# Row stages of a two-block transformer kernel: the first 128 tokens handled apart from the others

## The reference

```python
x = x + rmsnorm(mixed @ w_out[l], attn_post_norm[l])     # first row stage
h = rmsnorm(x, ffn_pre_norm[l])                          # goes into w_up
...
y = (gelu(gate) * up) @ w_down[l]
x = x + rmsnorm(y, ffn_post_norm[l])                     # second row stage
h = modulate(rms_norm(x, norm_gains[0, 0]), ...)         # goes into w_qkv of the second block
```

## Time and profile before

| | before |
|---|---|
| median of 3 runs | 1040.23 us (1039.89 to 1041.08) |
| the profiled execution | 1041.97 us |
| its span, first to last instruction | 1040.2 us |
| PE busy | 1023.5 us (98%) |
| DVE busy | 813.5 us (78%) |
| ACT busy | 592.8 us (57%) |
| POOL busy | 165.7 us (16%) |
| mean granted TensorE clock | 0.997 |

### The profile page before, as it was taken

How to read it: one execution, slowest core, us unless ns; L and a number is a source line. 1 busy time by engine, 2 the same in 40 slices (tenths; PEclk the granted TensorE clock), 3 DMA queues, 4 the chain that set the end, 5 groups by cost and what they waited for, 6 DMA issues and landing times.

```text
span 1040.2 us, 18418 instructions
## 1 busy us (share of the span) xinstructions
PE 1023.5 (98%) x7440; PEld 955.2 (92%) x7440; DVE 813.5 (78%) x1399; ACT 592.8 (57%) x1027; POOL 165.7 (16%) x172
## 2 busy tenths in 40 slices
PE   8999999999999999999999999999999999999997
PEld 7988898999889997999999889988999899999987
DVE  5878799999997987588999798885668676674553
ACT  5688676665446666565444455544465566544443
POOL 1000134333101200032122011201100123111010
PEclk8999999999999999999999999999999999999999
DMA  9733356776894433457997887554434536774441
GB/s 363 263 121 123 122 195 243 271 290 249 324 390 176 163 123 122 159 190 279 373 381 299 318 312 281 203 174 150 158 127 165 200 128 235 282 268 152 168 167 41
DMA packets 34129, 227.44 MB, mean 219 GB/s; under 512 B 3795, under 2 KB 4092, under 8 KB 10492
## 3 DMA queue, kind: packets, MB, share of 16 engines
q1 hardware_dynamic: 33596, 223.63, 57.5%
q0 software_dynamic: 448, 2.63, 0.6%
HBM read 225.19 MB, written 2.63 MB: 219 GB/s over the span
## 4 chain that ended last, share of the span: by engine, by line
PE 86%; DVE 9%; ACT 2%; issue 1%; DMA 0%; POOL 0%; POOLq 0%; SPq 0%; ACTq 0%; DVEq 0%
PE psum L1513 16%; PE psum L1514 16%; PE psum L1515 16%; PE psum L1557 9%; PE psum L1558 5%; DVE w_lo L2269 3%; PE psum L1582 2%; PE psum L1585 2%; PE psum L1584 2%; PE psum L1933 2%; PE psum L1935 2%; PE psum L1934 2%; ACT w_hi L827 1%; PE psum L1724 1%; DVE arena L2593 1%; PE psum L1616 1%
## 5 line engine op out<-in xcount | busy, mean ns | idle before, releaser
L2269 DVE TENSOR_TENSOR w_lo<-raw,w_hi 128x1024 fp32r<-128x1024 f32 (+2 forms) x340 | 387.1, 1160 | 134.3 <-ACT w_hi L827 129.2
L827 ACT ACTIVATE w_hi<-raw 128x1024 fp32r<-128x1024 f32 (+2 forms) x340 | 333.4, 996 | 210.0 <-PE psum L1515 82.6
L1513 PE MATMUL psum<-h_hi,w_hi 128*128 128x256 f32 (+1 forms) x1144 | 324.5, 284 | 5.6 <-DVE w_lo L2269 2.7
L1514 PE MATMUL psum<-h_hi,w_lo 128*128 128x256 f32 (+1 forms) x1144 | 321.0, 281 | 0.0
L1515 PE MATMUL psum<-h_lo,w_hi 128*128 128x256 f32 (+1 forms) x1144 | 320.6, 280 | 0.0
L1513 PEld LDWEIGHTS psum<-h_hi,w_hi 128*128 128x128 f32 x1144 | 215.4, 188 | 9.4 <-DVE w_lo L2269 5.6
L1515 PEld LDWEIGHTS psum<-h_lo,w_hi 128*128 128x128 f32 x1144 | 215.4, 188 | 0.0
L1514 PEld LDWEIGHTS psum<-h_hi,w_lo 128*128 128x128 f32 x1144 | 214.7, 188 | 0.7 <-issue 0.7
L1513 PE MATMUL psum<-hid,w_hi 128*128 128x256 f32 (+1 forms) x532 | 152.6, 287 | 0.5 <-DVE w_lo L2269 0.2
L1514 PE MATMUL psum<-hid,w_lo 128*128 128x256 f32 (+1 forms) x532 | 149.9, 282 | 0.0
L1515 PE MATMUL psum<-hid,w_hi 128*128 128x256 f32 (+1 forms) x532 | 149.9, 282 | 0.0
(11 more groups left out here) (302 smaller groups left out, 1371.3 us busy)
## 6 DMA issues: line engine op xcount, KB each, us to landing
arena<-in_ada SPq DMA_DIRECT2D x48, 1024.0 KB, 6.1
raw<-in_gu SPq DMA_DIRECT2D x44, 1024.0 KB, 6.9
raw<-in_ret_in SPq DMA_DIRECT2D x24, 1024.0 KB, 4.8
raw<-in_up SPq DMA_DIRECT2D x22, 1024.0 KB, 4.8
raw<-in_dn SPq DMA_DIRECT2D x32, 704.0 KB, 4.1
raw<-in_qkv SPq DMA_DIRECT2D x12, 1024.0 KB, 5.0
raw<-in_down SPq DMA_DIRECT2D x11, 1024.0 KB, 7.5
raw<-in_ret_o SPq DMA_DIRECT2D x8, 1024.0 KB, 4.8
```

The source lines that it names most:

```text
L827: nc.scalar.activation(w_hi[chunk % SPLIT_SLOTS][:, a:b], raw[chunk % RAW_SLOTS][:, a:b], ACT.Copy)\
L1513: nc.tensor.matmul(out, w[0], hc, start=start, stop=False, skip_group_check=True)
L1514: nc.tensor.matmul(out, w[1], hc, start=False, stop=False, skip_group_check=True)
L2269: tt(w_lo[s][:, a:b], raw[chunk % RAW_SLOTS][:, a:b], w_hi[s][:, a:b].bitcast(F32), ALU.subtract)\
```

## The change

The factor of the first 128 tokens is made as soon as their two pieces are squared: `row_mean`, `row_roots` and `row_rstd` are each called once for r = 0 and once for r = 1, on one column instead of two. The refinement has the factor 1.5 and -0.5 folded in, still four small steps. The diagonal of r = 0 moves from DVE to ACT (`first_diag`), that of r = 1 stays on DVE. PE turns all eight blocks of r = 0 first and then all of r = 1; 14 filler matmuls stand ahead in stage 0, and none ahead and 4 between the two turns in stage 1, instead of 18 ahead. The PSUM places of the turned tiles are dealt out anew, tile 7 shares a bank with tile 0 and waits for its reading, and DVE is told after tiles 0, 2, 4, 6 and 7. In `rows_by_gains` ACT squares tile 0 after rounding tile 1, tile 1 after 2, tile 2 after 4, tile 3 after 5, and tiles 4 to 7 after 7, instead of each right behind its own.

```diff
 def turned_rows(k):
-    return (tra + att)[k // 2][:, k % 2 * S:k % 2 * S + S]
+    bank, at = ((tra[0], 0), (tra[1], 0), (tra[1], S), (att[0], 0), (att[0], S), (att[1], 0), (att[1], S), (tra[0], S))[k]
+    return bank[:, at:at + S]
+TURN_ENDS = (0, 2, 4, 6, 7)
...
+def row_roots(stage, r):
+    act.wait_ge(row_ms, 2 * stage + r + 1)
+    nc.scalar.activation(row_stat[:, 6 + r:7 + r], row_stat[:, r:r + 1], ACT.Sqrt).then_inc(row_root, 1)
+def first_diag(stage):
+    act.wait_ge(row_factor, stage + 1)
+    nc.scalar.activation(row_diag_of(0), ident[:, :], ACT.Identity, scale=row_stat[:, 24:25]).then_inc(row_diag, 1)
 def mix_squares(ph):
     for r in range(2):
+        if r:
+            row_roots(0, 0)
         for n in range(2):
...
-    act.wait_ge(row_ms, 1)
-    nc.scalar.activation(row_stat[:, 6:8], row_stat[:, 0:2], ACT.Sqrt).then_inc(row_root, 1)
+    first_diag(0)
+    row_roots(0, 1)
 def row_squares(ph, i):
     for r in range(2):
+        if r:
+            row_roots(stage, 0)
         for n in range(2):
             if r == 1 and n == 1:
+                first_diag(stage)
                 act.wait_ge(half_done, 2 * (ph.chunk0 + ph.n))
...
+    row_roots(stage, 1)
 def rows_by_gains(i):
+    squares = {1: (0,), 2: (1,), 4: (2,), 5: (3,), 7: (4, 5, 6, 7)}
     for k in range(DT):
...
-        square(i, k)
+        for n in squares.get(k, ()):
+            square(i, n)
 def turn_rows(ph, i):
-    keep_busy(18, att[1])
+    if stage == 0:
+        keep_busy(14, att[1])
+    else:
+        pe.wait_ge(row_copied, 2)
+    pe.wait_ge(row_diag, 2 * stage + 1)
+    for k in range(DT):
+        turn(k, 0)
+    if stage:
+        keep_busy(4, sco[0])
     units_done(pe, ph.unit0 + ph.units)
...
+    pe.wait_ge(row_diag, 2 * stage + 2)
     for k in range(DT):
+        if k == DT - 1:
+            pe.wait_ge(row_x, DT * stage + 1)
+        ins = turn(k, 1)
+        if k in TURN_ENDS:
             ins.then_inc(row_turned, 1)
 def row_copies(ph, i):
     for r, n in ((0, 0), (0, 1), (1, 0)):
+        if r:
+            row_mean(ROW_STAGE[i], 0)
+            row_rstd(ROW_STAGE[i], 0)
 def row_residual(ph, i, gain_):
-    stt(row_stat[:, 0:2], row_stat[:, 28:30], EPS, row_stat[:, 30:32], ALU.add, ALU.add).then_inc(row_ms, 1)
-    refine(row_root, stage + 1, row_stat, 2)
-    for r in range(2):
-        ts(row_diag_of(r), ident[:, :], row_stat[:, 24 + r:25 + r], -0.5, ALU.mult, ALU.mult).then_inc(row_diag, 1)
+    if stage == 0:
+        row_rstd(0, 0)
+    row_mean(stage, 1)
+    row_rstd(stage, 1)
+    ts(row_diag_of(1), ident[:, :], row_stat[:, 25:26], 1.0, ALU.mult, ALU.mult).then_inc(row_diag, 1)
...
 def add_rows(c, first, r, g):
     for n in range(2):
+        if (c, r, n) == (3, 1, 1):
+            row_mean(0, 0)
```

More of the change, by code:

```diff
@@ L361, in build @@
             "rows_done", "row_sq", "row_copied", "row_ms", "row_root", "row_diag", "row_turned", "row_x"))
+        row_factor = sem("row_factor")
         settled_conv, settled_qk = sem("settled_conv"), sem("settled_qk")
@@ L1073, in row_squares @@
                                              scale=D ** -0.5, accum_out=row_stat[:, at:at + 1]).then_inc(row_sq, 1)
-                act.wait_ge(row_ms, stage + 1)
-                nc.scalar.activation(row_stat[:, 6:8], row_stat[:, 0:2], ACT.Sqrt).then_inc(row_root, 1)
+                row_roots(stage, 1)
                 leave(nc.scalar.activation(row_of(1, 1), row_bank(ph, 1, 1)[:, :], ACT.Copy), ph.unit0 + 1)
             def rows_by_gains(i):
+                squares = {1: (0,), 2: (1,), 4: (2,), 5: (3,), 7: (4, 5, 6, 7)}
                 for k in range(DT):
@@ L1943, in turn_rows, with turn @@
                 stage = ROW_STAGE[i]
-                keep_busy(18, att[1])
+                rows = mix_rows if stage == 0 else e0["y"]
+                def turn(k, r):
+                    return nc.tensor.matmul(turned_rows(k)[:, r * P:(r + 1) * P], rows[:, r * D + k * P:r * D + (k + 1) * P],
+                                            row_diag_of(r), start=True, stop=True)
+                if stage == 0:
[7 more added lines that the diff above has]
+                    keep_busy(4, sco[0])
                 units_done(pe, ph.unit0 + ph.units)
@@ L1947, in turn_rows @@
                     pe.wait_ge(row_y, 2)
-                else:
-                    pe.wait_ge(row_copied, 2)
-                rows = mix_rows if stage == 0 else e0["y"]
+                pe.wait_ge(row_diag, 2 * stage + 2)
                 for k in range(DT):
-                    for r in range(2):
[L1953 to L1957, removed]
+                    if k == DT - 1:
+                        pe.wait_ge(row_x, DT * stage + 1)
+                    ins = turn(k, 1)
+                    if k in TURN_ENDS:
                         ins.then_inc(row_turned, 1)
@@ L2339, in norm_h, with row_mean, row_rstd @@
                 tiles_of(i)
+            def row_mean(stage, r):
+                dve.wait_ge(row_sq, 4 * stage + 2 * (r + 1))
+                stt(row_stat[:, r:r + 1], row_stat[:, 28 + r:29 + r], EPS, row_stat[:, 30 + r:31 + r], ALU.add, ALU.add).then_inc(row_ms, 1)
+            def row_rstd(stage, r):
+                m, s, a, f = (row_stat[:, at + r:at + r + 1] for at in (0, 12, 18, 24))
+                dve.wait_ge(row_root, 2 * stage + r + 1)
+                link(nc.vector.reciprocal(s, row_stat[:, 6 + r:7 + r]))
+                link(stt(a, s, -0.5, m, ALU.mult, ALU.mult))
+                link(tt(a, a, s, ALU.mult))
+                ins = stt(f, a, 1.5, s, ALU.add, ALU.mult)
+                if r == 0:
+                    ins.then_inc(row_factor, 1)
+                else:
+                    link(ins)
             def row_copies(ph, i):
                 for r, n in ((0, 0), (0, 1), (1, 0)):
+                    if r:
+                        row_mean(ROW_STAGE[i], 0)
+                        row_rstd(ROW_STAGE[i], 0)
                     dve.wait_ge(row_sq, 4 * ROW_STAGE[i] + 2 * r + n + 1)
@@ L2353, in row_residual @@
                 stage = ROW_STAGE[i]
-                dve.wait_ge(row_sq, 4 * (stage + 1))
-                stt(row_stat[:, 0:2], row_stat[:, 28:30], EPS, row_stat[:, 30:32], ALU.add, ALU.add).then_inc(row_ms, 1)
-                refine(row_root, stage + 1, row_stat, 2)
-                for r in range(2):
-                    ts(row_diag_of(r), ident[:, :], row_stat[:, 24 + r:25 + r], -0.5, ALU.mult, ALU.mult).then_inc(row_diag, 1)
+                if stage == 0:
[3 more added lines that the diff above has]
+                ts(row_diag_of(1), ident[:, :], row_stat[:, 25:26], 1.0, ALU.mult, ALU.mult).then_inc(row_diag, 1)
                 def rest_of(k):
@@ L2365, in row_residual @@
                 for k in range(DT):
-                    if k % 2 == 0:
-                        dve.wait_ge(row_turned, DT // 2 * stage + k // 2 + 1)
+                    if k == 0 or k - 1 in TURN_ENDS:
+                        dve.wait_ge(row_turned, len(TURN_ENDS) * stage + (k + 3) // 2)
                     cut = slice(k * S, (k + 1) * S)
```

## The result

The changed kernel took 1048.53 us (median of 6 runs, 1046.95 to 1049.64), the kernel before 1040.65 us in the same rounds (6 runs, 1039.89 to 1043.87): ratio 1.0068, 95% interval 1.0057 to 1.0080, so 7.1 us slower by the ratio. Forecast was 1043.6 us with a range up to 1046.5. The sign and the first mechanism, sums that wait for POOL, came out as forecast. The clock, which the forecast expected to be kept, fell as well, and the time lies outside the range.

The account below looks back on a forecast made before the run. PE bounds most of the kernel, but DVE sets the pace from 321 to 347 us. Late sums in stage 0 (+1.7 to +2.2) and stage 1 (+1.2 to +1.75), taken as +3.4 on 1040.23, gave 1043.6 us, range 1041.3 to 1046.5.

Parts of the forecast that it names:

- the first mechanism: Both row stages: PE's sums of squares wait for POOL's additions, +1.7 to +2.2 us in stage 0, +1.2 to +1.75 in stage 1.
- Part 1: Stage 1, early factor of r = 0: factor at about 320.2, ACT's diagonal 0.4 us, diagonal of r = 1 about 322.45.
- Part 2: PE's split turn: first residual 0.5 us earlier in stage 1 (bounds 0.3 to 0.65), 0.1 in stage 0 (0 to 0.2).
- Part 3: Moved squares: last rest some 0.5 us sooner, but POOL's late additions meet DVE's splits; sums late, +3.4 us over both stages.
- the first of the two orders: POOL's fourth addition ahead of DVE's first split: split runs 7.53 to 8.67 from the first residual; stage 1 sums at 334.5.
- clock kept: The forecast's own case: both stages late by the sums, no clock fall, 1042.2 to 1044.6 us; chance 0.50.
- (b): PE stands still around the sums and the clock falls: +1.2 to +2.9 us per stage hit, 1044.8 to 1049; chance 0.17.
- (a): Sums not late, POOL slipping between DVE's work or PE's head start covering it: about 1040.2, at best 1038.6; chance 0.20.
- its weaker form: POOL's additions undisturbed by the splits, ending at 332.97 in stage 1 and 133.9 in stage 0: about 1040.2, no change.
- (c): Second addition comes ahead of the fifth rest, last rounding 0.8 us later in that stage: 1044.4 to 1045.2; chance 0.10.
- (d): Early turn brings nothing because ACT's diagonal holds the fourth square: +0.5 us, inside the forecast's range, no chance of its own.
- Slack at chunk 3: Sign: PE's 0.49 us wait for DVE at chunk 3 should stay; if gone, DVE had room and the forecast is wrong.

Follow-up runs that it names:

- e1: Changed kernel with each square again right behind its own rounding (early factor and split turn stay): 1040.54 us, ratio 0.9990 to the kernel before.
- e6: Changed kernel with DVE's split of chunk 1 in both row stages reading one operand from PSUM (that part's product wrong): 1043.35 us, ratio 1.0019.
- e2: Kernel before with only the new places of the squares: 1047.79 us, ratio 1.0072.
- e10: The changed kernel itself, unedited, run again beside e11: 1048.48 us, ratio 1.0064 to the kernel before.
- e3b: Changed kernel with 4 filler matmuls ahead of chunk 1 and 14 ahead of the sums in both row stages: ratio 1.0043 to the kernel before.
- e11: Same kernel as e3b (fillers while PE waits), timed again beside the changed kernel: 1044.36 us, ratio 1.0023 to the kernel before.
- e5: Changed kernel with squares trailing their rounding by one tile only (tiles 6 and 7 behind 7): 1043.25 us, ratio 1.0009.
- e7: e1 with 2 fillers instead of 4 between the two turns of stage 1: ratio 0.9994 to the kernel before.
- e9: Same version as e7 (e1 with 2 fillers in stage 1), timed again in more rounds: ratio 0.9997 to the kernel before.
- e4: Changed kernel with three POOL additions in the row stages, PE summing tiles 4 to 7 itself (20 one-column passes instead of 8): 1045.14 us, ratio 1.0029.
- e8: e4 with 6 fillers of 256 columns ahead of the one-column passes in each row stage: 1043.79 us, ratio 1.0037.

## Why the prediction was right on the late sums and wrong on the clock

**Part 1, the early factor: right to 0.1 us.** Forecast in before's time: factor at 320.2, first turn 320.73, second diagonal 322.45, second turn 323.0, first residual 323.46. Measured, less the 2.31 us by which the trace of after stands later: 320.16, 320.71, 322.38, 323.05, 323.47. ACT's new diagonal took 0.40 us, as taken between its two neighbours. This timeline row of ACT is the term that the earlier trace rows could only bound:

```profile
322.47 0.40 ACT L1057 ACTIVATE diag<-ident,row_stat 128x128 f32<-128x128 f32 x1 [0.24 <-DVE row_stat L2379]
```

**Part 2, the turn: right.** The residual is 0.50 earlier in stage 1 (forecast 0.5) and 0.16 in stage 0 (forecast 0.1, bound 0.2).

**Part 3, the squares: right.** The split of chunk 1 starts at 332.83, in before's time 330.52 (forecast 330.5); of this, 0.49 us is due to the squares in each stage (after against e1; forecast 0.5). POOL was first by 0.06 us, as in the first of the two orders. The forecast had the split wait its turn; in fact it starts and is stretched, 1.76 us for 1.22, and the fifth addition ends 0.60 us behind the split's end (335.19 against 334.59), just the distance of the earlier trace rows. The same again for the second split and the sixth addition (336.86 against 336.27). Sums in before's time: 334.68 in stage 1 (forecast 334.5 or 335.0) and 135.55 in stage 0 (forecast 135.4 or 135.95). Together +3.24 against +3.4.

The trace agrees with the Trainium skill (SBUF — State Buffer, "Who interferes with whom") on the kind of conflict, and e6 shows that it goes away with a PSUM operand. The forecast set DVE's loss of 0.49 us against the 0.74 of a whole addition and made a difference of it, but a loser can only be held for what is left of the other's operation when it starts. Read so, both engines pay alike in this trace: the first split starts with 0.68 us of the addition left and loses 0.54 (1.76 instead of 1.22), the fifth addition starts with 0.94 us of the split left and loses 0.79 (1.53 instead of 0.74). The row that seems to break the order, POOL's at 462.92 ahead of two splits, starts inside a DVE operation with two SBUF operands (L2601, 462.76 to 463.23), and so second.

**The step that failed: "clock kept" as the likeliest case, and (b) at 0.17.** The forecast itself laid out PE's work around the sums: 0.8 us of waiting, 0.46 of work, another 1.8 to 2.3 of waiting (in the trace of after 0.57 and 0.55 of waiting, then 1.73 in both stages). It also had the earlier trace rows, in which PE was busy for 2.58 of 3.45 us and half clock followed. The layout leaves PE far less busy than the row in which the clock had fallen, so by the rows at hand (b) deserved far more than 0.17, and nothing was put forward against it. It happened in both stages of the trace of after, in both of e2 and in both of e10, in each case behind a PE wait of 1.7 us, and in none of e3b, e11, e5, e6, e1, e7 and e9, where no PE wait around the sums is longer than 0.7 us. In e4 and e8 it fell in one stage of two without such a wait, so a long wait is not the only thing that brings it. The price per stage in (b) was right to 0.15 us: +1.2 to +2.9 forecast, +1.06 and +1.28 measured for one stretch, and 1.28 + 1.67 = 2.95 for the double one in e10. With (b) in both stages the forecast's own sum is 3.4 + 2 x 1.2 = 5.8, with the longer stretches up to 9; measured 5.0 in the profiled span and 7.1 and 6.7 in the two ratios. The range, which took in only the nearer half of (b), ended at 6.3 us of loss (1046.5 less 1040.23).

So the traced execution, with one stretch in each stage, accounts for 5.6 us, and the ratio has 7.1. The other five executions of after took 1.9 us more in the median (1048.86) at a mean clock of 0.991 to 0.993. More stretches behind the sums, as in e10, would give that, but it was not seen, and the mean clock can't show it: e10's traced execution has the same 0.994 as after's, with three stretches behind the sums where after has two there and one at the start. Nor is the start always counted: in e10 six fillers at 12.14 us take 1.65 us, as long as in before at half clock (11.09 us), while its windows show 1.00.

**The other rivals.** (a), sums not late, is refuted by the rows, and its weaker form by e6: even with splits that leave POOL alone, PE waits 0.6 us. (c), a later last rounding, did not occur: in stage 1 it starts at 331.88, in before's time 329.57, to the digit as forecast, and the last rest starts 0.35 (stage 0) and 0.69 us (stage 1) earlier. (d) is refuted by the residuals of part 2.

**Slack at chunk 3.** The forecast said it was wrong if this gap was gone. In stage 1 0.17 us of it is left and in stage 0, where it was 0.31, nothing: with PE at half speed behind the sums, DVE catches up. With the clock held it is back (0.48 and 0.31 in e11). So here the gap that went was a sign of the clock, not of room on DVE.

**What stays open.** Executions of one kernel differ by more than the terms that are sought: those of the kernel before range from 1039.8 to 1044.9 us in the last comparison. The traces show where. The last matmul by rows of stage 0 comes at 119.06 to 120.93 us, the wider distance in `w_up` is there or not (1.5 us), and from the first matmul of the attention to the end it is either 685.7 to 686.0 us or 687.2 to 687.3. e3b and e11 are one kernel and differ by 2.37 us in the span, 0.91 ahead of stage 0 and 1.46 behind the attention, with the row stages alike to 0.02. That is as much as the 2.4 and 4.5 us of the late sums in the two comparisons lie apart; both lie around the 3.2 that the distances give. What makes these terms come and go I didn't look for.

## What to carry to other kernels

Work moved away from the engine that sets the pace is not free if another engine's results are due at a fixed point: lay out the last consumer first, and ask who runs beside the moved work and reads the same memory. Where a forecast has PE stand still for a microsecond or two around a short piece of work, look for stretches of the trace behind which the clock had fallen, and don't leave the fall a small chance without a reason: here it came in all six stages traced with such waits, and its price comes on top of the wait. In this kernel the squares were cheapest to add while the pacing engine worked on small tiles, and not once it had reached its long instructions.

## What the runs showed of the hardware

- A DVE subtraction of 128x1024 with two SBUF operands takes 1.22 us alone and 1.76 with a POOL addition begun 0.06 us before it; the next addition, begun inside it, takes 1.53 instead of 0.74. Either engine loses what is left of the other's operation when it starts, less some 0.15 us. With a PSUM operand on DVE the three additions of the row take 2.49 us instead of 4.08.
- Fillers during the waits kept the clock at 1.00 behind them in four of four stages (e3b, e11), with the waits' end unchanged (sums at 15.88 against 15.87). In this kernel that was worth 4.1 us of 1048.5 in the direct comparison.
- Twenty one-column passes with PE busy throughout were followed by half clock in one stage of e4 and not in the other, and so in e8: PE's busy time in the windows does not tell which.
- The first 3.41 us at half clock cost 1.06 to 1.28 us, the next 1.67 (e10, stage 1).
- The mean granted clock does not tell how often the clock fell behind the row stages: it was 0.994 both with two stretches there (after) and with three (e10).
